# Second scan direction's transposed inverses kept in the other half of the partitions

## The reference, cut to what matters

```python
def step(S, inp):                       # one token, one head; S is 64x64
    r_t, w_t, k_t, v_t, a_t, b_t = inp
    sa = jnp.einsum('bhij,bhj->bhi', S, a_t)
    S = S * w_t[:, :, None, :] + sa[..., None] * b_t[:, :, None, :] + v_t[..., None] * k_t[:, :, None, :]
    y = jnp.einsum('bhij,bhj->bhi', S, r_t) if emit else None
    return S, y
...
S_f, y_f = rwkv_scan(states0[0], r, decay[0], k_dir[0], v, -kk, b_dir[0], False, emit)
S_b, y_b = rwkv_scan(states0[1], r, decay[1], k_dir[1], v, -kk, b_dir[1], True, emit)
```

## Time and profile before

| what | value |
|---|---|
| median of three runs | 3101.37 us (3097.13 to 3104.19) |
| span of the profiled execution | 3091.2 us |
| own time of the profiled execution beside the span | not given; the median is 10.2 us above the span |
| PE busy | 2874.3 us, 93% |
| DVE, ACT, POOL busy | 49%, 31%, 25% |
| mean granted TensorE clock | 0.975 |

### The profile page before, as it was taken

How to read it: one execution, slowest core, us unless ns; L and a number is a source line. 1 busy time by engine, 2 the same in 40 slices (tenths; PEclk the granted TensorE clock), 3 DMA queues, 4 the chain that set the end, 5 groups by cost and what they waited for, 6 DMA issues and landing times. The chain is left out here.

```text
span 3091.2 us, 61066 instructions
## 1 busy us (share of the span) xinstructions
PE 2874.3 (93%) x25648; PEld 2134.9 (69%) x25648; DVE 1512.4 (49%) x2768; ACT 964.4 (31%) x2248; POOL 771.8 (25%) x977
## 2 busy tenths in 40 slices
PE   6989998999998998999999989998999798999999
PEld 4968787886563786764588856645888576458674
DVE  5654636454433854541464246427833774265552
ACT  2021213122432124551221137511212574112561
POOL 3312223130013430011222214225531432244000
PEclk8999999999999999999999989999999899999999
DMA  6230100001332112121211152020111311212100
GB/s 225 81 113 19 39 4 16 17 32 59 110 103 101 55 55 96 56 83 41 83 52 47 66 188 77 11 95 34 55 55 55 124 55 56 87 47 89 58 1 28
DMA packets 108049, 206.16 MB, mean 67 GB/s; under 512 B 21795, under 2 KB 25394, under 8 KB 107264
## 3 DMA queue, kind: packets, MB, share of 16 engines
q1 hardware_dynamic: 107504, 201.36, 18.6%
q0 software_dynamic: 272, 0.89, 0.1%
HBM read 186.91 MB, written 15.54 MB: 65 GB/s over the span
## 5 line engine op out<-in xcount | busy, mean ns | idle before, releaser
L665 PE MATMUL psum<-weights,h_t 128*128 128x256 f32 x1488 | 352.0, 379 | 0.8 <-ACT p_u_u L749 0.8
L665 PEld LDWEIGHTS psum<-weights,h_t 128*128 128x128 f32 x1488 | 279.6, 190 | 38.5 <-ACT p_u_u L749 1.2
L1299 DVE TENSOR_REDUCE neg_max<-psum 128x1 f32<-128x768 f32 (+1 forms) x192 | 159.8, 864 | 220.4 <-PE psum L1169 174.8
L665 PE MATMUL psum<-z_l,x_tiles 128*128 128x256 f32 x816 | 192.8, 379 | 0.0
L665 PEld LDWEIGHTS psum<-z_l,x_tiles 128*128 128x128 f32 x816 | 155.0, 190 | 21.1
L1862 PE MATMUL psum<-weights,q_l 128*128 128x512 f32 x384 | 166.5, 592 | 0.0
L760 ACT ACTIVATE square<-psum 128x512 f32<-128x512 f32 (+1 forms) x80 | 45.0, 565 | 378.5 <-DVE psum L1017 242.0
L1190 PE MATMUL psum<-eye,prob 128*128 128x128 f32 x832 | 135.9, 286 | 11.3 <-DVE prob_t L1317 3.9
L1346 POOL TENSOR_TENSOR z_l<-z_l,inv_total 128x128 f32<-128x128 f32 x80 | 31.9, 399 | 428.7 <-DVE inv_total L1310 428.7
L1264 ACT ACTIVATE prob<-psum,neg_max 128x768 f32<-128x768 f32 (+1 forms) x160 | 129.7, 816 | 18.6 <-DVE neg_max L1299 12.4
L1862 PEld LDWEIGHTS psum<-weights,q_l 128*128 128x128 f32 x384 | 72.2, 190 | 87.1 <-issue 87.1
(11 more groups left out here) (445 smaller groups left out, 6175.9 us busy)
## 6 DMA issues: line engine op xcount, KB each, us to landing
weights<-in_ada_w_dram SPq DMA_DIRECT2D x30, 2048.0 KB, 8.0
weights<-in_a_w_in_dram SPq DMA_DIRECT2D x10, 2048.0 KB, 8.7
weights<-in_b_w_in_dram SPq DMA_DIRECT2D x8, 2048.0 KB, 9.2
weights<-in_c_w_in_dram SPq DMA_DIRECT2D x8, 2048.0 KB, 9.1
weights<-in_w_in_dram SPq DMA_DIRECT2D x6, 2048.0 KB, 7.7
x_aside<-x_tiles SPq DMA_DIRECT2D x24, 512.0 KB, 2.6
x_tiles<-x_aside SPq DMA_DIRECT2D x4, 3072.0 KB, 12.8
weights<-in_a_w_out_dram SPq DMA_DIRECT2D x4, 2048.0 KB, 8.0
```

Of the source, the lines that this page charges most:

```text
L665: last = pe.matmul(dst, lhs[:, k, :], rhs[k // 2][:, k % 2, :], start=k == 0, stop=k == KH - 1)
L1299: last = dve.tensor_reduce(neg_max[:, i % 4, m:m + 1], score(i, m, 0, keys), AX, ALU.max, negate=True)
```

## The change

Direction 1's `inv_t`, its crossed products and `x_s` are put into the other partition half (head h in partitions of half 1-h); `inv` stays. `other_half` and `solved_in` name the half. Direction 0 then runs on tiles (0,0) and (1,1), direction 1's crossed and straight products, and in the scan W and U, on (0,1) and (1,0). The turned products read and write one half for both directions and stay on (0,0) and (1,1). Batches of the inverse are now three, each 4 chunks of both directions (nb = 3), so a step has 16 calls of each kind. Since a VectorE operation can't cross partitions, direction 1's `inv_t` is begun by a product of its own: job `t1`.

```diff
+def other_half(s):
+    return slice(64 - s.start, 128 - s.start)
+def solved_in(d, s):
+    return s if d == 0 else other_half(s)
...
             jobs.append(("n1", d, chunks, b["a_f"], b["b_f"], low + "1", b["inv"]))
+            if d == 1:
+                jobs.append(("t1", d, chunks, b["b_f"], b["a_f"], up + "1", b["inv_t"]))
...
+                        to = other_half(s) if name == "t1" else s
+                        last = pe.matmul(pr.bank(i % 8)[to, width * n:width * n + width], left[s, d, cols], rhs,
                                          start=True, stop=True)
...
-                if name == "nt":
+                if name == "nt" and d == 0:
...
-    batches = [(d, seg) for d in range(2) for seg in range(2)]
-    steps = [(li, m, bi) for li, m in enumerate(LEVELS[1:]) for bi in range(4)]
+    batches = [(0, 4), (4, 8), (8, 12)]
+    nb, each = len(batches), 4
+    steps = [(li, m, bi) for li, m in enumerate(LEVELS[1:]) for bi in range(nb)]
...
+        def x_ps(i, d):
+            return pr.bank(2 * (i % 2) + d)[:, 0:CH * each]
+        def straight_ps(i, d):
+            return pr.bank(4 + 2 * (i % 2) + d)[:, 0:HALF * each]
+        def turned_ps(i, d):
+            return pr.bank(4 + 2 * (i % 2))[:, HALF * each * (1 + d):HALF * each * (2 + d)]
...
+                src = pr.bank(2 * (i % 2), 2).rearrange("p (d n) -> p d n", d=2)[:, :, 0:CH * each]
+                act.activation(x_s[:, :, a:e, :], src.rearrange("p d (c t) -> p d c t", t=CH), ACT.Copy)\
+                    .then_inc(*x_out.tick())
...
+                for c in range(a, e):
+                    for d in range(2):
+                        for s in halves:
+                            out = x_ps(i, d)[solved_in(d, s), CH * (c - a):CH * (c - a) + CH]
+                            last = pe.matmul(out, n_m[li % 2][s, d, c, :], b["inv"][s, d, c, :], start=True, stop=True)
...
+                            to = solved_in(d, s)
+                            out = straight_ps(i, d)[s, HALF * (c - a):HALF * (c - a) + HALF]
+                            pe.matmul(out.rearrange("p (b m) -> p b m", m=m), b["inv_t"][to, d, c, :],
+                                      half_of(x_s[to, d, c, :], m, d), start=True, stop=True)
...
+                            out = turned_ps(i, d)[s, HALF * (c - a):HALF * (c - a) + HALF]
+                            last = pe.matmul(out.rearrange("p (b m) -> p b m", m=m), x_s[s, d, c, :],
+                                             half_of(b["inv_t"][s, d, c, :], m, 1 - d), start=True, stop=True)
...
+                    to = solved_in(d, s) if i == W else s
...
-                    last = pe.matmul(pr.bank(6)[s, cols(d)], b["inv_t"][s, d, chunk(d), :], w_s[s, d, :],
+                    at = solved_in(d, s)
+                    last = pe.matmul(ps(U, d)[s], b["inv_t"][at, d, chunk(d), :], w_s[at, d, :],
```

More of the change, by code:

```diff
@@ L2972, in _ @@
                     continue
-                d, seg = batches[bi]
-                a, e = chunks(seg)
+                a, e = batches[bi]
                 if li >= 2:
[L2976 to L2979, removed]
+                    pool.wait_ge(*x_done.at(nb * (li - 2) + bi + 1))
+                for d in range(2):
+                    name = ("up" if d == 0 else "low") + str(m)
+                    last = pool.tensor_tensor(n_m[li % 2][:, d, a:e, :], b["m_ab_t"][:, d, a:e, :],
+                                              wide(masks[:, MASKS.index(name), :], 1, e - a), ALU.mult)
+                last.then_inc(*masked.tick())
         @block.vector
@@ L2983, in _ @@
             for i, (li, m, bi) in enumerate(steps):
[L2984 to L2987, removed]
+                a, e = batches[bi]
                 dve.wait_ge(*p_done.at(i + 1))
-                if li < final:
-                    dve.tensor_tensor(t, t, products, ALU.add)
-                dve.tensor_tensor(tt, tt, turned, ALU.add).then_inc(*added.tick())
+                for d in range(2):
+                    t, tt = blocks(b["inv"][:, d, a:e, :], m, d), blocks(b["inv_t"][:, d, a:e, :], m, 1 - d)
+                    products, turned = (x.rearrange("p (c b m) -> p c b m", c=each, m=m)
+                                        for x in (straight_ps(i, d), turned_ps(i, d)))
+                    if li < final:
+                        dve.tensor_tensor(t, t, products, ALU.add)
+                    last = dve.tensor_tensor(tt, tt, turned, ALU.add)
+                last.then_inc(*added.tick())
         @block.scalar
@@ L3003, in _, with half_of, crossed @@
+                act.activation(x_s[:, :, a:e, :], src.rearrange("p d (c t) -> p d c t", t=CH), ACT.Copy)\
+                    .then_inc(*x_out.tick())
         @block.tensor
         def _(pe):
-            def products(bank, lhs, rhs, i, half=None):
+            halves = [slice(64 * h, 64 * h + 64) for h in range(2)]
+            def half_of(x, m, odd):
+                return x.rearrange("p (b two m) -> p b two m", two=2, m=m)[:, :, int(odd), :]
+            def crossed(i):
                 li, m, bi = steps[i]
-                d, seg = batches[bi]
-                a, e = chunks(seg)
-                width = CH if half is None else CH // 2
+                a, e = batches[bi]
@@ L3010, in products @@
                 for c in range(a, e):
[L3011 to L3018, removed]
@@ L3019, in products @@
-                return last
+                    for d in range(2):
+                        for s in halves:
+                            out = x_ps(i, d)[solved_in(d, s), CH * (c - a):CH * (c - a) + CH]
+                            last = pe.matmul(out, n_m[li % 2][s, d, c, :], b["inv"][s, d, c, :], start=True, stop=True)
+                last.then_inc(*x_done.tick())
             def finish(i):
                 li, m, bi = steps[i]
-                d = batches[bi][0]
+                a, e = batches[bi]
@@ L3069, in products @@
                 for d, s in pairs:
+                    to = solved_in(d, s) if i == W else s
                     for j, term in enumerate(terms):
                         lhs, rhs = term(d, s)
-                        last = pe.matmul(ps(i, d)[s], lhs, rhs, start=start and j == 0,
+                        last = pe.matmul(ps(i, d)[to], lhs, rhs, start=start and j == 0,
                                          stop=stop and j + 1 == len(terms))
@@ L3125, in _ @@
                     dve.wait_ge(*y_done.at(n - 1 - CC))
-                dve.tensor_copy(u_s[:, n % 2, :, :], pr.bank(6)[:, 0:P].rearrange("p (d i) -> p d i", d=2))\
+                dve.tensor_copy(u_s[:, n % 2, :, :], both(U))\
                     .then_inc(*u_out.tick())
```

51 lines of the change are left out of this document (25 added, 26 removed).

## The result

The changed kernel takes 3108.4 us (median of 9 runs, 3103.3 to 3121.2), the kernel before beside it 3097.1 (9 runs, 3091.4 to 3104.2): a ratio of 1.0048, 95% interval 1.0030 to 1.0065. It is half a per cent slower where 1.6% faster was forecast. Its profiled span is 3115.7 us, 24.5 longer than the 3091.2 of before. The profiled execution is one of the slower of the nine (3117.5 us), so these 24.5 us are more than the 11.3 between the medians.

What follows compares the result with a forecast made beforehand. TensorE's tiles were taken to bound the inverse and matrix stage, latency the scan. Inverse -50, matrix stage +5.6 and scan -9.6 gave -54.0 us: span 3037.2, with 10.2 kept on top 3047.4 us; range 3040 to 3090.

Steps and rivals of the forecast that it cites:

- So the tile is the limit, not the issue: Inverse: each tile takes one load and one MATMUL per 0.058 us, so two more tiles at work would help.
- 26.5 us: Inverse: TensorE's time per head pair after the change, against 39.2 worked out for before.
- Rival 2: Issue already at its limit, a record every 0.029 us whatever the tile; inverse gains nothing, 3097 or somewhat lower; chance 15%.
- Crossed and straight on four tiles 0.465 each: Inverse: a phase of 16 crossed or straight calls takes 0.465 us on four tiles, against 0.93 on two.
- Rival 3: Off-diagonal tiles can't work beside those sharing rows and outputs, and TensorE drains between: 3107 to 3276 us; chance 8%.
- rival 1: Inverse: issue at 0.035 us a call makes crossed and straight phases 0.56 us, not 0.465; 3058 us; chance 20%.
- the 25 ns between MATMULs: Inverse: a least distance between MATMUL starts, from the skill; crossed and straight would take 0.80, the sum 3083 us.
- rival 4: Inverse: new waits, `x_s` or the adds late in most steps, 0.3 us a step, 18 us in all; 3065; chance 7%.
- The granted clock, "I give it no case": Thinner scan: a clock fall would cost, but it was 1.00 in all three windows, so no chance was given.
- Scan, -9.6 us: Scan: W's and U's groups on four tiles each end 0.10 us earlier, 9.6 us gained over four pairs.
- Matrix stage, `t1`, +5.6 us: Matrix stage: `t1` adds 24 calls a pair at 0.058 us, 1.4 us a pair, 5.6 us in all.
- the inverse should have brought 50 us: Inverse: 12.5 us gained per head pair from crossed and straight products on four tiles, 50 us for four pairs.

Runs made afterwards that it cites:

- run 5: The changed kernel without the inverse's straight products and the additions that take them (inverses come out incomplete): 3058.5 us, ratio 0.9884 to the kernel before.
- run 6: The kernel before with one more single-column product, in an idle tile, after every second call of the inverse: 3176.2 us, ratio 1.0261.
- run 7: The changed kernel with straight products 64 columns wide and 12 unread products in each scan step that emits nothing: 3086.1 us against 3094.3 before, ratio 0.9975.

## Why the prediction was wrong

- **"So the tile is the limit, not the issue"** is the step that failed. The tile was the limit by 3.72 to 3.64 us per 128 records, so by next to nothing. Starts 0.01 apart and eight loads within 0.05 are bursts out of a block that had arrived; I took the pace of a burst for one that can be kept up. No row of a burst could show the mean rate of the stream. A row that I didn't quote could have warned me: 11 packets on the instruction queue in the inverse before, one every 3.8 us, and nowhere in that trace two less than 3.4 us apart, where the forecast needed one every 2.5 (26.5 us for 10.5 blocks). Runs 5 and 6 show the limit from both sides.
- **Rival 2** (a record every 0.029 us on the mean, whatever the tile, 3097) had the size right, as 3.64 / 128 is 0.0284, and got 15%. My argument against it, that a queue stood filled behind the tiles, was no argument: TensorE runs at full pace until the block ends.
- **"Crossed and straight on four tiles 0.465 each"**: right, 0.44 (for 30 of 32 records) to 0.49 in the rows above. Rival 3, tiles that block or drain each other, is dead, and so are rival 1 and the 25 ns between MATMULs that the prediction cites from the Trainium skill ("TensorE: Matmul & The Clock Gate", section "Wait — 56ns, not 53.3ns?"): 30 records in 0.44 us are 0.015 each. By rival 4 ScalarE's or VectorE's results would come late; in the second inverse the long idle times stand at "issue", and TensorE's busy time of 29.4 us is near the 26.5 worked out.
- **The granted clock, "I give it no case"**: it had one, and it made the difference between no change and slower. The changed kernel does the same work in less busy time, and TensorE is granted 1.2 GHz for 76 us in four inverses and 65 in four scans, where before it had 2.4 throughout these stages. That it was 1.00 in them before was no evidence for a kernel in which TensorE does the same work in less busy time.
- **Scan, -9.6 us**: right in its mechanism. An emitting step at the full clock takes 2.36 us (461.45 to 463.81 in the second pair, loads of the state's products) for the forecast 2.32 and 2.525 before. With the clock held (run 7, with the extra work) the scan is 1.6 us a pair shorter than before, 1.9 where it never fell, for the forecast 2.4.
- **Matrix stage, `t1`, +5.6 us**: too much. The first pair grew by 0.6 us, not 1.4: its calls are on tiles off the diagonal and probably run beside the others, which wasn't tried by itself. VectorE's time fell from 14.6 to 14.1. The second pair's 2.0 holds a spell of the lower clock (0.92).
- In the profile's own sum: the inverse should have brought 50 us and the supply allows some 2 to 3 a pair (38.2 to 39.8 against 40.8 to 41.6); the lower clock took these back, so that the inverses came out 10.7 us longer.

The Trainium skill names this fetch and takes it for hidden. "Runtime: NRT & Kernel Launch", section "Instruction fetch mechanics", says that each engine's instruction memory is refilled in blocks of 16 KiB, 256 instructions, and that crossing a block is "mostly hidden" because an engine issues more slowly than blocks arrive. The size of the block agrees with the stops here. The rest holds for two tiles at 3.72 us a block and fails for the changed inverse, where TensorE is through a block in about 2.5 us (404.90 to 407.43): there 0.4 to 1.4 us of each block stand open.

## What to carry to other kernels

Before making TensorE's calls faster, count its instructions in the stage (four for each product in fp32) and look at the instruction queue: if the stage's length is already blocks of 256 times some 3.7 us, then by runs 5 and 6 fewer instructions make it shorter, not free tiles, fewer columns or a better order. Where a change leaves TensorE with less to do between waits, look at the granted clock of the stage, and if it falls, compare with a version that has wider products or some that nobody reads; here wider products and 192 idle ones that were put in turned a loss of 0.5% into a gain of 0.25%.

## Hardware behaviour that was not expected

- TensorE runs out of instructions: in starved inverses at the full clock the 16 KB packets start 3.3 to 4.6 us apart, 3.6 to 3.8 on a stage's mean, each of them on its way for 0.9 to 1.5 us, and TensorE goes on 1.2 to 1.6 us after one has landed.
- A wait that is long satisfied isn't free between products: two of them ahead of a call made the pace 0.131 us a call where it was 0.058, at the same full clock.
- The lower clock level appeared without any change in instructions: in one execution the inverse took 38.2 us in the first pair and 48.1 in the second.
